# Final layer norms of five token tiles moved from behind the FFN into its second group's turns

## The reference

```python
x = layer_norm(ALPHA * x + jnp.einsum('btm,md->btd', mix, w_out), ln1_g, ln1_b)
hid = jax.nn.silu(jnp.einsum('btd,df->btf', x, wg)) * jnp.einsum('btd,df->btf', x, wu)
return layer_norm(ALPHA * x + jnp.einsum('btf,fd->btd', hid, wd), ln2_g, ln2_b)
# layer_norm(x) = (x - mean) * rsqrt(var + LN_EPS) * g + b
```

## Time and profile before

| | us |
|---|---|
| median of 3 runs | 3131.69 |
| lowest to highest | 3128.27 to 3135.31 |
| the profiled execution | 3134.1 |
| its span in the profile | 3132.3 |

### The profile page before, as it was taken

One profiled execution on the slowest core, in us unless ns is written; L12 is line 12 of the kernel. 1 busy time (PEld: TensorE's weight loads), 2 busy tenths in 40 slices (PEclk: granted clock), 3 DMA queues, 4 the chain that ended last, 5 costly groups with the idle time before them and its releaser, 6 DMA issues. The chain is left out here.

```text
span 3132.3 us, 58397 instructions
## 1 busy us (share of the span) xinstructions
PE 2920.8 (93%) x20464; PEld 2660.8 (85%) x20464; DVE 2143.3 (68%) x3877; ACT 1247.7 (40%) x2422; POOL 1739.4 (56%) x1358
## 2 busy tenths in 40 slices
PE   7979997999999999999889699989999999999996
PEld 6956666887999999999889566668879999899996
DVE  6757676667666677777755577766576666877777
ACT  3324334445333344444333333444453333444442
POOL 2323333436766668788622233434376666788886
PEclk9989998999999999999889799989999999999998
DMA  4321114543222213232332211156432222132222
GB/s 171 126 83 42 50 39 157 156 161 113 87 82 83 80 58 105 98 103 94 123 115 94 78 48 41 32 166 182 133 116 81 81 83 85 67 101 100 100 87 89
DMA packets 175821, 304.91 MB, mean 97 GB/s; under 512 B 56080, under 2 KB 97296, under 8 KB 175344
## 3 DMA queue, kind: packets, MB, share of 16 engines
q1 hardware_dynamic: 165088, 271.70, 26.7%
q0 software_dynamic: 10576, 31.14, 2.5%
HBM read 248.34 MB, written 50.38 MB: 95 GB/s over the span
## 5 line engine op out<-in xcount | busy, mean ns | idle before, releaser
L2771 PE MATMUL PS<-xoh,woph 128*128 128x320 f32 (+1 forms) x2464 | 735.6, 299 | 14.6 <-issue 11.4
L2772 PE MATMUL PS<-xol,woph 128*128 128x320 f32 (+1 forms) x2464 | 733.4, 298 | 0.0
L2773 PE MATMUL PS<-xoh,wopl 128*128 128x320 f32 (+1 forms) x2464 | 732.2, 297 | 0.0
L1494 POOL TENSOR_TENSOR wopl<-T,woph 128x512 fp32r<-128x512 f32 x348 | 517.6, 1505 | 147.4 <-ACT woph L1958 147.4
L2771 PEld LDWEIGHTS PS<-xoh,woph 128*128 128x128 f32 x2464 | 466.2, 189 | 18.4 <-issue 13.5
L2772 PEld LDWEIGHTS PS<-xol,woph 128*128 128x128 f32 x2464 | 466.3, 189 | 0.2
L2773 PEld LDWEIGHTS PS<-xoh,wopl 128*128 128x128 f32 x2464 | 466.0, 189 | 0.0
L1441 POOL TENSOR_TENSOR Pl<-Pf,Ph 128x256 fp32r<-128x256 f32 (+5 forms) x174 | 219.0, 1265 | 387.2 <-DVE Ph L2353 387.2
L2771 PE MATMUL PS<-hidh,wdh 128*128 128x320 f32 (+1 forms) x1408 | 419.9, 298 | 11.5 <-DVE hidl L2620 7.8
L1958 ACT ACTIVATE woph<-T 128x512 fp32r<-128x512 f32 x348 | 217.0, 631 | 521.4 <-DVE T L2615 303.9
L2773 PE MATMUL PS<-hidh,wdl 128*128 128x320 f32 (+1 forms) x1408 | 419.2, 298 | 0.0
(11 more groups left out here) (476 smaller groups left out, 6654.9 us busy)
## 6 DMA issues: line engine op xcount, KB each, us to landing
ru<-in_W_FF SPq DMA_DIRECT2D x88, 512.0 KB, 4.0
rd<-in_W_FF SPq DMA_DIRECT2D x176, 256.0 KB, 2.6
rg<-in_W_FF SPq DMA_DIRECT2D x82, 512.0 KB, 4.2
sqt_scratch<-sqTs POOLq DMA_DIRECT2D x18, 512.0 KB, 3.9
hc<-out_H SPq DMA_DIRECT2D x18, 512.0 KB, 3.7
out_H<-yo POOLq DMA_DIRECT2D x18, 512.0 KB, 3.0
dkraw<-in_CKVT SPq DMA_DIRECT2D x16, 520.0 KB, 4.7
QS<-sqt_scratch SPq DMA_DIRECT2D x16, 512.0 KB, 3.5
```

What stands on the lines that cost most here:

```text
L1494: pool.tensor_tensor(wopl[k][:, :, :], w_whole(w, k, first), f(woph[k][:, :, :]), ALU.subtract)\
L2771: pe.matmul(out, wh, mh, start=start, stop=False)
L2772: pe.matmul(out, wh, ml, start=False, stop=False)
L2773: return pe.matmul(out, wl, mh, start=False, stop=stop)
```

## The change

Tiles 0 to 4 get their final norm inside turns 12 to 21 of each layer, two turns for each tile: the first (12, 14, 16, 18, 20) turns, moves, measures and scales, the second (13, 15, 17, 19, 21) applies the root and stores. After down product 5 PE makes 4 + 4 transposes into `Tb[0]` and `Tb[1]`, each half after DVE's addition from that bank; ACT copies both halves back into `acc0` in place; PE's down products 6 and 7 wait for these copies. DVE then measures and scales from SBUF (before, from PSUM). All bias work of these tiles is on DVE, and their stores are still issued by POOL. The tail keeps tiles 5 to 9. Group 1's operands `xoh`, `xol`, `xsum` lie at a smaller pitch, which frees room for `lnd` and a buffer `y_early`; `lnd` is loaded in turn 11. `winraw` of layer 1 gets another place. Layer 1's first tile loads no longer wait for the last transposes. The loops over group 1's turns are written out on PE, DVE, ACT and POOL (SP keeps its loop). `xo_hi` and the copies share a semaphore, now `f_moved`.

```diff
-        X_PITCH = 4 * 4 * HALF_G[0]
+        X_PITCH = [4 * 4 * h for h in HALF_G]
...
+        winraw.append(m("winraw_next", [P, KD, INW]))
+        m = Map(common + 14 * X_PITCH[1])
         lnd = m("lnd", [P, 2 * D])
+        y_early = m("y_early", [P, D])
...
-        LAST_T = {5: 2, 8: 3, 11: 4, 14: 5}
-        LAST_STATS = {2: 1, 5: 2, 8: 3, 11: 4, 14: 5}
-        AFTER_DOWN = 6
+        EARLY_TILES = 5
+        LAST_T = {9: 5, 13: 6}
+        LAST_STATS = {10: 5, 15: 6}
+        AFTER_DOWN = 7
...
@@ SP, start of layer 1 @@
-                    sp.wait_ge(S("d_T"), A(l - 1, TILES - 1) + 1)
+                    sp.wait_ge(S("ln_norm"), norms_done(l - 1, EARLY_TILES - 1))
                     for i in range(2):
                         sp.wait_ge(S(f"yo_out{i}"), yo_done(l - 1, i))
-                    sp.wait_ge(S("f_lo"), PRODUCTS * TURNS * l)
-                    sp.wait_ge(S("f_dlo"), 4 * TURNS * l)
...
@@ SP, second group @@
-                with sp.Fori(0, PAIRS - 1) as j:
+                turn(0, c, False)
+                sp.wait_ge(S("f_prod"), PRODUCTS * (TURNS * l + PAIRS))
+                load_params(sp, l, "D")
+                with sp.Fori(1, PAIRS - 1) as j:
                     turn(j, c, False)
                 turn(PAIRS - 1, c, True)
                 sp.wait_ge(S("f_prod"), PRODUCTS * TURNS * (l + 1))
-                load_params(sp, l, "D")
...
@@ POOL, turn @@
+                        if i == 9 and y_turn_of(no) is not None:
+                            ln_root(pool, qD(l, y_turn_of(no)), P)
+                        if i == 9 and y_end_of(no) is not None:
+                            y = y_end_of(no)
+                            pool.wait_ge(S("ln_out"), qD(l, y) + 1)
+                            pool.dma_start(H[l + 1, cols(y), :], y_early[:, :]).then_inc(S(f"yo_out{y % 4}"), 16)
...
@@ POOL, tail @@
-                for t in range(TILES + 1):
+                for t in range(EARLY_TILES, TILES + 1):
...
@@ ACT @@
+                def y_move(t, half):
+                    act.wait_ge(S("d_T"), y_turned(l, t, half))
+                    act.activation(y_rows(t, half), Tb[half][:, :].rearrange("p (k n) -> p k n", n=P), ACT.Copy)\
+                       .then_inc(S("f_moved"), 1)
...
+                        if i == 6 and y_turn_of(no) is not None:
+                            for half in range(2):
+                                y_move(y_turn_of(no), half)
...
-                with act.Fori(PAIRS + 1, TURNS - 1) as j:
-                    turn(j, c, 1)
-                turn(TURNS - 1, c, 1, TURNS - 1)
+                for j in range(PAIRS + 1, TURNS):
+                    turn(j, c, 1, j)
...
@@ DVE @@
+                def y_stats(t):
+                    q = qD(l, t)
+                    dve.wait_ge(S("f_moved"), y_moved(l, t, 1))
+                    dve.wait_ge(S("ln_out"), q - 3)
+                    for half in range(2):
+                        ins = dve.bn_stats(stats[q % 2][:, 6 * half:6 * half + 6], y_rows(t, half))
...
+                def y_scale(t):
+                    q = qD(l, t)
+                    if t:
+                        dve.wait_ge(S(f"yo_out{(t - 1) % 4}"), yo_done(l, t - 1))
+                    else:
+                        params(dve, (l, "D"))
+                    dve.scalar_tensor_tensor(out=y_early[:, :].rearrange("p (k n) -> p k n", n=P), in0=y_rows(t),
+                                             scalar=mv[ln_slot(q)][:, 0:1],
+                                             in1=lnd[:, 0:D].rearrange("p (k n) -> p k n", n=P),
+                                             op0=ALU.subtract, op1=ALU.mult).then_inc(S("ln_norm"), 1)
...
+                        if i == 3 and y_end_of(no) is not None:
+                            y_norm(y_end_of(no))
+                        if i == 6 and y_turn_of(no) is not None:
+                            y_stats(y_turn_of(no))
+                        if i == 11 and y_turn_of(no) is not None:
+                            y_scale(y_turn_of(no))
...
-                params(dve, (l, "D"))
                 hid_lo(TURNS - 1, c, 1)
-                last_stats(0)
...
@@ PE @@
+                def y_turn(t, half):
+                    for k in range(4):
+                        ins = pe.transpose(Tb[half][:, k * P:k * P + P], acc_rows(t, 4 * half + k), ident[:, :])
+                    ins.then_inc(S("d_T"), 1)
...
+                                elif u in (6, 7) and y_turn_of(no) is not None:
+                                    pe.wait_ge(S("f_moved"), y_moved(l, y_turn_of(no), u - 6))
...
+                                if u == 5 and y_turn_of(no) is not None:
+                                    for half in range(2):
+                                        pe.wait_ge(S("f_y"), Q(j - 1, c, DOWNS, u + half))
+                                        y_turn(y_turn_of(no), half)
...
-                y_T(0)
-                y_T(1)
```

More of the change, by code:

```diff
@@ L401, in program @@
         m = Map(after_w)
[L402 removed]
+        winraw = [m("winraw", [P, KD, INW])]
         assert m.at <= after_kv
@@ L529, in program @@
         m = Map(common)
-        X_PITCH = 4 * 4 * HALF_G[0]
-        xoh = [Map(common + 2 * i * X_PITCH)(f"xoh{i}", [P, 4 * HALF_G[0]], F32R) for i in range(7)]
-        xol = [Map(common + (2 * i + 1) * X_PITCH)(f"xol{i}", [P, 4 * HALF_G[0]], F32R) for i in range(7)]
-        xsum = [Map(common + (2 * i + 1) * X_PITCH)(f"xsum{i}", [P, 4 * HALF_G[0]]) for i in range(7)]
+        X_PITCH = [4 * 4 * h for h in HALF_G]
+        xoh, xol, xsum = ([[Map(common + (2 * i + a) * X_PITCH[g])(f"{name}{g}_{i}", [P, 4 * HALF_G[g]], dt) for i in range(7)]
+                           for g in range(2)] for name, a, dt in (("xoh", 0, F32R), ("xol", 1, F32R), ("xsum", 1, F32)))
         after_x = common + 2 * KD * TOK * 4
-        assert common + 14 * X_PITCH <= after_x
+        assert common + 14 * X_PITCH[0] <= after_x
         m = Map(wo_at)
@@ L808, in qD, with y_turned, y_moved, y_rows @@
             return 2 * TILES + 2 * TILES * l + t
-        LAST_T = {5: 2, 8: 3, 11: 4, 14: 5}
-        LAST_STATS = {2: 1, 5: 2, 8: 3, 11: 4, 14: 5}
-        AFTER_DOWN = 6
+        EARLY_TILES = 5
+        LAST_T = {9: 5, 13: 6}
+        LAST_STATS = {10: 5, 15: 6}
+        AFTER_DOWN = 7
         NORM_DVE = (7, 9)
-        NORM_ACT = [t for t in range(TILES) if t not in NORM_DVE]
+        NORM_ACT = [t for t in range(EARLY_TILES, TILES) if t not in NORM_DVE]
         def last_bank(u, g):
             return (Tb[0], Tb[1], PS[:, 2 * BANK:3 * BANK], PS[:, 5 * BANK:6 * BANK])[u % 4][:, 0:HALF_G[g]]
+        def y_turned(l, t, half=1):
+            if t < EARLY_TILES:
+                return (TILES + EARLY_TILES) * l + 2 * t + half + 1
+            return (TILES + EARLY_TILES) * l + EARLY_TILES + t + 1
+        def y_moved(l, t, half):
+            return XO(l, 1, X_BY_ACT[1][-1]) + 1 + 2 * t + half + 1
+        def y_rows(t, half=None):
+            k = slice(0, KD) if half is None else slice(4 * half, 4 * half + 4)
+            return acc0[:, k, cols(t)]
+        def y_turn_of(no):
+            return None if no is None or no <= PAIRS or (no - PAIRS) % 2 == 0 or no >= TURNS - 1 else (no - PAIRS) // 2
+        def y_end_of(no):
+            return y_turn_of(no - 1) if no is not None else None
         def acc_rows(t, k):
@@ L1535, in _ @@
                 turn(PAIRS, c, PAIRS)
-                with pool.Fori(PAIRS + 1, TURNS - 1) as j:
-                    turn(j, c)
-                turn(TURNS - 1, c, TURNS - 1)
+                for j in range(PAIRS + 1, TURNS):
+                    turn(j, c, j)
                 down_lo(TURNS - 1, c, 1)
@@ L2728, in _ @@
                 turn(PAIRS - 1, c, 0, PAIRS - 1)
-                turn(PAIRS, c, 1, PAIRS)
-                turn(PAIRS + 1, c, 1, PAIRS + 1)
-                with dve.Fori(PAIRS + 2, TURNS - 1) as j:
-                    turn(j, c, 1)
-                turn(TURNS - 1, c, 1, TURNS - 1)
+                for j in range(PAIRS, TURNS):
+                    turn(j, c, 1, j)
                 def last_stats(t):
                     r, q = rows(t), qD(l, t)
-                    dve.wait_ge(S("d_T"), A(l, t) + 1)
+                    dve.wait_ge(S("d_T"), y_turned(l, t))
                     ln_stats(dve, q, Sb[t % 2], r)
-                    if t >= 4:
+                    if t - 4 >= EARLY_TILES:
                         dve.wait_ge(S(f"yo_out{t % 4}"), yo_done(l, t - 4))
@@ L3352, in _ @@
                 turn(PAIRS, c, 1, PAIRS)
-                with pe.Fori(PAIRS + 1, TURNS) as j:
-                    turn(j, c, 1)
+                for j in range(PAIRS + 1, TURNS):
+                    turn(j, c, 1, j)
                 def y_T(t):
                     r = rows(t)
-                    if t < 5:
-                        pe.wait_ge(S("f_y"), DOWNS * (TURNS * l + PAIRS))
-                    else:
-                        pe.wait_ge(S("f_y"), DOWNS * (TURNS * (l + 1) - 1) + (KD if t < 7 else DOWNS))
-                    if t == 0:
```

(9 more changed lines are left out.)

40 lines of the change are left out of this document (27 added, 13 removed).

## The result

The changed kernel takes 3136.72 us (median of 20 runs, 3132.00 to 3144.91); before, in the same job, 3132.27 us (20 runs, 3123.76 to 3139.49). The ratio of after to before is 1.0018, with a 95% interval of 1.0010 to 1.0026. By the ratio it is slower by about 5.6 us, where 14.2 us less were forecast: outside the range, and on the other side.

A forecast was written before the change was run, and what follows sets the result against it. PE was taken to bound group 1's turns, POOL's row of ten tiles layer 1's tail. Saved 12.4 + 20, less 12, 5 and 1.2 paid, gave 14.2 us: 3117 us, range 3108 to 3129.

The forecast's parts named there:

- Tails: Ends of both layers: no wait for `lnd` and five tiles fewer save 20 us between layers, 12.4 us in layer 1.
- Transposes: PE in the turns, behind down product 5: 1.2 us for each tile, 12 us in all.
- ACT's copies and the statistics in step 6: Turns: ACT's two copies cost nothing; DVE's statistics (1.6 us) fill idle time, nothing, up to 0.3.
- Scaling at step 11: DVE in the turns, 1.27 us reading SBUF: slack behind it covers this, nothing, up to 0.5.
- the prediction's paragraph on the shared port: DVE with two SBUF inputs and POOL lock a shared port; the later starter is blocked for the whole instruction.
- Second norm step at step 3: DVE before down product 4: 1.2 us of work in 1.4 of slack; PE loses 0.5 us per tile, 5 in all.
- the first rival: Turns take the gain back: DVE's norm steps lose a whole POOL instruction, 29 us paid, 3129.5 us; chance 0.16.
- POOL's store issue and root: POOL in the turns: root 0.57 and issue 0.6 to 0.9 us, on 27.20 of 33 us busy, cost nothing.
- Clock: PE after standing still before the tail's down products: slower clock costs 0.6 us per tail, 1.2 in all.
- The rival of the written-out code: PE stops for instructions in the 20 written-out turns, 1.8 us each, 36 us: 3153.7 us; chance 0.06.

The follow-up runs named there:

- run 1: Changed kernel with all ten tiles' norms back in the tails, early `lnd` load and written-out turns kept: ratio 0.9976 to the kernel before.
- run 6: Four kernels on top of run 4: transposes split (0.9936), left out (0.9935), split with statistics in step 7 (0.9943), split with another tail order (0.9946).
- run 7: Changed kernel with each norm step in the turns replaced by two one-input statistics instructions, outputs of tiles 0 to 4 left out: ratio 0.9966 to the kernel before.
- run 5: Changed kernel with only the second norm step moved, from step 3 to step 6 of the odd turns: ratio 0.9999 to the kernel before.
- run 4: Changed kernel with all norm work moved to places where DVE and POOL both idle, everything still computed: 3109.42 us against 3133.17 for the kernel before.
- run 3: Changed kernel with POOL's root and store issue one step sooner, in step 8 instead of 9: ratio 0.9973 to the kernel before.
- run 8: Five kernels: run 1 plus a POOL computation (0.9980, 0.9973) or store issue (1.0003 twice) in odd turns; changed kernel with early stores issued by SP (0.9988).

## Why the prediction was wrong

- **Tails: right.** 21.7 and 12.8 us saved, for 20 and 12.4. In run 1 the earlier load alone makes them 2.4 and 4.2 us shorter.
- **Transposes: right.** 1.18 us for 1.2. ACT's copies and the statistics in step 6 cost nothing, as said; run 6 shows by how little.
- **Scaling at step 11, "nothing, up to 0.5": wrong, 0.94 us.** I took 1.27 us, the time from the tail, and counted the slack behind it. It took 2.17, since it reads two SBUF tensors beside a busy POOL, as the prediction's paragraph on the shared port says itself; yet I used the medians of the earlier trace rows only for the second norm step. The same rows stood for this one. Run 7 shows that 1.3 us would have fitted.
- **Second norm step at step 3, "0.5": mis-sized, 0.94 us** (runs 5 and 7). It took 2.32 us against 1.28 alone (run 4), so it was held for 1.0 us, most of a POOL instruction; I had counted on half of one, and priced a whole one at 1.3 for the first rival.
- **POOL's store issue and root, "nothing": wrong, and the real surprise.** I asked whether POOL had room for them. It has, being busy for 27 of 34 us. But POOL's place in time decides whether DVE's old instructions are held. The root adds to the first wait (run 3); the issue makes the third, 1.1 us in four of five odd turns (runs 3 and 8).
- **Clock: nothing lost in the profiled run.** PE stood still for 2.19 us, and the granted clock stayed at 1.00 (window 3101.50 to 3105.50). In run 4, after the same 2.19 us, it fell to the lower level for 3 us and 14 matmuls took 0.22 instead of 0.12 us, 1.4 us in all. In the profiles with this stop of 2.19 us the matmuls slowed down so in 8 of 22 tails. So 0.6 in each tail, with a bound of 1.6, was a fair price, and that the profiled run paid nothing was luck.

In all 0.5 us was set for DVE and POOL for each tile, and they took 2.7: 22 us over the ten tiles. That is more than the whole miss of 18.6 us in the table: 38.9 us were paid for 17, against 34.5 saved for 32.4 and 1.2 of clock not paid. The first rival, "the turns take it back", named the mechanism but counted two places, not three, and 29 us for 38.9. It also misquotes the forecast: a tile costs 1.2 + 0.5 us in the sum, not "1.2 + 1.5". And 0.12 and four times 0.1 are 0.52 us, not 0.56, which changes nothing. The rival of the written-out code is refuted by run 1.

## What to carry to other kernels

Before you put an instruction into a stage with little slack, ask which memory it reads there and who runs beside it: the scaling took 1.27 us from PSUM and 2.2 us from SBUF beside a busy POOL, and a norm step from SBUF 1.28 us with POOL idle. On a helper engine with spare time, an added instruction can still hurt by shifting those behind it against another engine's. When one of three separate prices is found, move the work into a stretch where both engines idle and read the turn's length, not the total time: 4.5 us for eleven turns were plain to see where the total time spread over about 20.

## Not expected of the hardware

- A DMA issue on POOL (0.56 to 0.62 us in the trace, whether for 8 KB or 0.5 MB) directly ahead of a row of three POOL instructions keeps a DVE instruction with two SBUF inputs waiting behind the whole row: 2.78 to 2.89 us, once 3.16, against 1.51 behind a POOL computation of 0.58 us and 0.43 alone.
- BATCH_NORM_STATS2 on SBUF took the same 0.67 us beside POOL's row (run 7) and without it (run 4), while TENSOR_SCALAR over 1024 columns, also with one SBUF input, took 1.64 and 1.78 us beside it.
- After the same 2.19 us of idle time PE's clock stayed at full speed in 14 tails and fell to half for about 3 us in 8.
